# An attention stage with its selections, a mixer split and a variance moved between blocks, and unread products added on TensorE

## The reference, cut to what matters

```
def diff_attention(q, k, v, lam, lam_init, subln_g):        # 4 heads, two maps each
        logits = einsum(qblk, k) * scale + bias              # distance bias, causal by chunks of 64
        p = softmax(where(allowed, logits, -inf))
        attn = p[:, :, 0] - lam * p[:, :, 1]
        return einsum(attn, v)
    o = rms_norm_2(o, subln_g) * (1.0 - lam_init)            # per head of 128

def dsa_attention(q, k, v, qi, ki, wi):                      # 4 heads of 64
        score = einsum(wi * idx_scale, relu(einsum(qi, ki)))
        _, sel = lax.top_k(score, topk)                      # 256 keys of each query
        ...softmax over the selected keys only
```

## Time and profile before

| | us |
|---|---|
| median of three runs | 2201.16 (2199.04 to 2201.55) |
| the profiled execution, its own time | 2189.69 |
| its span | 2187.9 |
| attention stage, first logits to last values | 1118.6 to 1336.5 |

### The profile page before, as it was taken

One profiled execution on the slowest core, in us unless ns is written; L12 is line 12 of the kernel. 1 busy time (PEld: TensorE's weight loads), 2 busy tenths in 40 slices (PEclk: granted clock), 3 DMA queues, 4 the chain that ended last, 5 costly groups with the idle time before them and its releaser, 6 DMA issues.

```text
span 2187.9 us, 25880 instructions
## 1 busy us (share of the span) xinstructions
PE 2108.8 (96%) x9834; PEld 1694.3 (77%) x9834; DVE 1100.7 (50%) x1708; ACT 746.3 (34%) x1189; POOL 178.4 (8%) x159
## 2 busy tenths in 40 slices
PE   5999999999999999999988998999999999999998
PEld 4888888878888887588855667878788888888877
DVE  7743463664234373878888764483412222222146
ACT  3311124432112443655755654242111111111133
POOL 1000002300000231012210000310000000000000
PEclk6999999999999999999978999999999999999999
DMA  8433333222111422101110002221111111111131
GB/s 301 144 118 95 105 105 87 77 68 70 45 48 48 135 81 87 51 21 29 49 39 1 1 1 106 87 77 53 54 49 48 45 56 50 40 48 58 46 127 77
DMA packets 222092, 154.75 MB, mean 71 GB/s; under 512 B 6565, under 2 KB 209462, under 8 KB 221878
## 3 DMA queue, kind: packets, MB, share of 16 engines
q1 hardware_dynamic: 215392, 134.53, 20.1%
q0 software_dynamic: 4608, 16.78, 2.3%
q10 hardware_dynamic: 2006, 2.31, 0.3%
HBM read 145.21 MB, written 8.39 MB: 70 GB/s over the span
## 4 chain that ended last, share of the span: by engine, by line
PE 82%; DVE 9%; ACT 6%; issue 2%; DMA 1%; POOL 0%; ACTq 0%; DVEq 0%; POOLq 0%; SPq 0%
PE pair L2084 36%; PE pair L2101 17%; PE pair L2534 8%; PE pair L2287 4%; PE pair L2142 3%; PE pair L2421 3%; ACT proj L996 2%; PE pair L2389 2%; PE pair L2320 2%; PE pair L2604 1%; PE pair L2403 1%; PE pair L2308 1%; PE pair L2113 1%; DVE act_region L1698 1%; DVE w_lo L1321 1%
## 5 line engine op out<-in xcount | busy, mean ns | idle before, releaser
L1327 DVE TENSOR_TENSOR w_lo<-w_raw,w_hi 128x1024 fp32r<-128x1024 f32 x101 | 123.8, 1225 | 672.0 <-ACT w_hi L780 671.8
L780 ACT ACTIVATE w_hi<-w_raw 128x1024 fp32r<-128x1024 f32 x102 | 108.2, 1061 | 804.1 <-PE pair L2084 623.0
L2084 PE MATMUL pair<-act_hi,w_hi 128*128 128x512 f32 x1168 | 361.3, 390 | 1.8 <-ACT v_all L936 1.8
L2084 PE MATMUL pair<-act_lo,w_hi 128*128 128x512 f32 x1168 | 359.6, 389 | 0.0
L2084 PE MATMUL pair<-act_hi,w_lo 128*128 128x512 f32 x1168 | 359.6, 389 | 0.0
L2084 PEld LDWEIGHTS pair<-act_hi,w_hi 128*128 128x128 f32 x1168 | 218.9, 188 | 48.8 <-ACT v_all L936 2.2
L2084 PEld LDWEIGHTS pair<-act_hi,w_lo 128*128 128x128 f32 x1168 | 219.2, 188 | 45.7
L2084 PEld LDWEIGHTS pair<-act_lo,w_hi 128*128 128x128 f32 x1168 | 219.2, 188 | 45.6
L2101 PE MATMUL pair<-act_hi,w_hi 128*128 128x512 f32 x608 | 243.9, 401 | 4.2 <-DVE act_lo L1340 2.0
L2101 PE MATMUL pair<-act_lo,w_hi 128*128 128x512 f32 x608 | 237.7, 391 | 0.0
L2101 PE MATMUL pair<-act_hi,w_lo 128*128 128x512 f32 x608 | 237.6, 391 | 0.0
(11 more groups left out here) (407 smaller groups left out, 3157.5 us busy)
## 6 DMA issues: line engine op xcount, KB each, us to landing
w_raw<-w_in SPq DMA_DIRECT2D x76, 512.0 KB, 3.7
w_raw<-w_out SPq DMA_DIRECT2D x48, 512.0 KB, 3.8
w_raw<-w_gu SPq DMA_DIRECT2D x48, 512.0 KB, 3.7
w_raw<-w_down SPq DMA_DIRECT2D x24, 384.0 KB, 3.0
act_region<-w_ada SPq DMA_DIRECT2D x16, 512.0 KB, 13.4
sq<-w_ada POOLq DMA_DIRECT2D x16, 512.0 KB, 3.8
sq_sum<-w_ada POOLq DMA_DIRECT2D x16, 512.0 KB, 4.9
yT<-x SPq DMA_DIRECT2D x8, 512.0 KB, 7.4
```

Of the source, the lines that this page charges most:

```text
L780: A(w_hi[s_][:], w_raw[s_][:], ACT.Copy).then_inc(hi_ready, 1)
L1327: v.tensor_tensor(w_lo[s_][:], w_raw[s_][:], f32(w_hi[s_][:]), ALU.subtract)\
L2084: i = mm(bank[pair][:, h * HALF:(h + 1) * HALF], w[slot][:, k, :], a[:, k, h * HALF:(h + 1) * HALF], start=(k == 0 and w is w_hi and a is ...
```

## The change

Four things are done, all around the attention loop.

1. Tiles 4, 5, 6 and 7 are selected in blocks 2, 3, 5 and 6 (`SELECT_IN`) instead of 0, 1, 2 and 3; the scratch is a row of `act_region` that is free then.
2. The mixer's split goes to block 7: ACT makes piece `it` at the end of iteration `it` of that block, behind `turned(k)`, and DVE its piece at the end of its own iteration, behind `combine(k)`, waiting for ACT's. The variance and scale of the first four blocks go from block 4 to block 7, too.
3. POOL makes `w_lo` of units 14 and 15 only after seven blocks' `c_out` (`c_taken`), and ACT makes `w_hi` of unit 15 behind the copy of unit 13. The loads of the next two weight pieces, which wait for POOL's parts, follow.
4. PE runs 14 more products, of 128x128 by 512 columns in FP32 (`keep_busy`), into half a bank pair that nothing reads: two ahead of the loop, and one in each of the twelve iterations of blocks 0 and 1, between `values(k-1)` and `turn(k)`.

```diff
+SELECT_IN = {2: 4, 3: 5, 5: 6, 6: 7}
...
-            for n in range(5, N_UNITS + 2):
+            for n in range(5, N_UNITS):
+                unit_lo(n)
+            pool.wait_ge(c_taken, TT - 1)
+            for n in range(N_UNITS, N_UNITS + 2):
                 unit_lo(n)
...
             for n in range(2, N_UNITS):
-                unit_hi(n + 2)
+                if n < N_UNITS - 1:
+                    unit_hi(n + 2)
+                else:
+                    act.wait_ge(unit_done, 1 + U_PROJ + n + 2)
...
+            unit_hi(N_UNITS + 1)
...
             exps(0)
-            for b in range(2):
-                for a in range(2):
-                    A(act_hi[:, b, a * HALF:(a + 1) * HALF], proj[:, S_AU + b, a * HALF:(a + 1) * HALF], ACT.Copy)\
-                        .then_inc(s_hi, 1)
             for k in range(N_ITEMS):
...
-                if k == 4 * ITEMS + 2:
+                if i == TT - 1 and it < MIX_CHUNKS:
+                    b, a = divmod(it, 2)
+                    act.wait_ge(sel_done, N_TS)
+                    A(act_hi[:, b, a * HALF:(a + 1) * HALF], proj[:, S_AU + b, a * HALF:(a + 1) * HALF], ACT.Copy)\
+                        .then_inc(s_hi, 1)
+                if k == 7 * ITEMS + 2:
                     act.wait_ge(ob_var, 1)
                     A(o_ss[:, tiles(0)], o_ss[:, tiles(0)], ACT.Sqrt).then_inc(ob_rstd, 1)
...
-                same = junk[:, 0:n] if i in EARLY_SEL else proj[:, S_AU, 0:n]
+                same = junk[:, 0:n] if i in EARLY_SEL else act_region[:, 0, 0:n]
...
-                if SEL0 + len(EARLY_SEL) + i < TT:
-                    select(SEL0 + len(EARLY_SEL) + i, it)
-                if k < MIX_CHUNKS:
-                    b, a = divmod(k, 2)
-                    dve.wait_ge(s_hi, SP_MIX + k + 1)
+                if i in SELECT_IN:
+                    select(SELECT_IN[i], it)
+                if i == TT - 1 and it < MIX_CHUNKS:
+                    b, a = divmod(it, 2)
+                    dve.wait_ge(s_hi, SP_MIX + it + 1)
...
-                if k == 4 * ITEMS + 1:
+                if k == 7 * ITEMS + 1:
                     ob_variance(0)
-                if k == 4 * ITEMS + 4:
+                if k == 7 * ITEMS + 4:
                     ob_scale(0)
+            dve.wait_ge(pool_lo, N_UNITS + 2)
+            dve.sem_inc(lo_ready, N_UNITS + 2)
...
+            def keep_busy():
+
+                mm(bank[2][:, half(1)], identity[:], dist_bias[:, half(0)], start=True, stop=True)
+
             logits(0)
             logits(1)
+            pe.wait_ge(dist_ready, 1)
+            keep_busy()
+            keep_busy()
             for k in range(N_ITEMS):
...
                 if k:
                     values(k - 1, groups_of(k - 1) - 1)
+                if i < 2:
+                    keep_busy()
                 if groups_of(k) == 2:
                     turn(k, 0)
```

More of the change, by code:

```diff
@@ L1777, in _ @@
                                     f32(act_hi[:, b, a * HALF:(a + 1) * HALF]), ALU.subtract).then_inc(s_lo, 1)
-                if k == MIX_CHUNKS:
-                    dve.wait_ge(pool_lo, N_UNITS + 2)
-                    dve.sem_inc(lo_ready, N_UNITS + 2)
                 if i and it == 0:
```

## The result

The changed kernel takes 2214.9 us (median of 4 runs, 2214.4 to 2216.2). The kernel before took 2201.0 beside it (2199.0 to 2201.6). The ratio is 1.0072, with a 95% interval from 1.0059 to 1.0085: slower by 0.7%. The profiled execution of the changed kernel took 2215.04 us, with a span of 2213.2.

A forecast was written before the change was run, and what follows sets the result against it. DVE bounds blocks 0 to 3, PE blocks 5 and 6. Terms -13.7 + 2.8 + 17.0 + 1.0 + 6.8 = +13.9 took the profiled 2189.7 to 2203.6; adding 11.5 gave 2215 us, range 2203 to 2226.

The forecast's parts named there:

- part 5: Block 7: PE, ACT and DVE run one after the other; +17.0 us, and +1.0 for POOL holding up DVE.
- part 6: Block 7: PE's clock falls behind each of four idle stretches, 1.7 us lost each; +6.8 us (0 to 10).
- parts 1 and 2: Entry gains 1.9 us, blocks 0 and 1 gain 7.1, with block 0 iterations of 1.9 us; 9.0 together.
- part 3: Blocks 2, 3, 4: smaller tiles gain 1.7 and 1.5 us in full, variance and scale leaving block 4 gain 1.5.
- part 4: Blocks 5 and 6: selection steps that don't fit DVE's free time cost +2.8 us (0 to 4).
- Behind attention: After the attention stage: clock full there, so nothing can move by this change; 0 us.
- The last step of the sum: Whole kernel: 2203.6 us for the profiled execution, plus 11.5 by which the kernel before's median exceeded its profile, gives 2215.
- Two of the prediction's signs: Block 7: DVE waits four times for ACT's split, 3 to 5 us each; the block grows by 18 to 25 us.
- That the waits cost no clock: Block 7: low clock passes while PE is idle; +7 us in sum, 2208 us; chance 0.14.
- Faster, only the first wait is paid: Block 7: PE pays 4.3 us once and the clock stays; -6.5 us, 2195 us; chance 0.13.
- that rival: Blocks 0 and 1: unread products don't hold the clock, some 10 us lost instead of 7 gained; 2232 us; chance 0.06.
- The draw: Attention: gains at upper bound (18) against block 7 at its lower (14); within 4 us of before; chance 0.12.

The follow-up runs named there:

- the attempt to steady that kernel: Kernel before with two unread products added in the last item of block 3: 2195.0 us, ratio 0.9992.
- the unchained kernel: Changed kernel, but DVE makes its four mixer pieces in one go in item 46, behind the last biased and the scale: 2187.6 us, ratio 0.9964.
- The two versions put together from the blocks: Changed kernel with DVE's mixer pieces in item 46, selections in blocks 0, 1, 3, 6, variance and scale in block 5: 2185.7 us with unread products, 2189.5 without.

## Why the prediction was right, and where it only seemed so

**Block 7's chain (part 5): right, with its sizes.** DVE waits four times for ACT's piece, 24.4 us in all, 4.2 to 8.0 each where the prediction had 3 to 5. PE's first `logits` behind the chain is 4.2 us late for 4.3. With the clock held full, the transposes of item 46 are 18.8 us late, where the prediction had 18.0 (17.0 + 1.0) for the copy of that item; the three products ahead of them may have a share in the 18.8. The variance and scale, counted at 1.2 and 0, cost 1.9 to 2.1 in block 7 of the kernels without the chain, at full clock; their share in the chained one no run shows. The 1.0 for POOL's lock was right in kind: the step of 0.22 us took 1.87 between POOL's 1297.20 and 1301.87, 1.65 longer, on an instruction of DVE with SBUF inputs only. The `biased` instructions beside it ran at 0.68 to 0.75 us, as they do without POOL, as the prediction took it. By the rule that it cited (the Trainium skill, SBUF — State Buffer, "Who interferes with whom"), the trace agrees. That the lock was gone from the entry shows too: 0.75 us where the earlier trace rows has 2.82:

```profile
1117.12 0.75 DVE L1688 SCALAR_TENSOR_TENSOR buf_b<-buf_b,cnt,junk 128x512 f32<-128x512 f32 x1
```

**The clock in block 7 (part 6): right in kind, too small, and wrong in form.** I had four falls of 1.7 us each, 6.8. Measured are 13.4 us by the two medians and 11.7 by the spans; by the stretches 11.8 in block 7 and 1.1 behind it. I took each fall to last as long as the one behind attention. By the same comparison (22.6 us late for the last transposes of item 46 with the falls, 18.8 without) the first three cost 3.8 us together. The fourth, behind a stand of 4.17 us, lasted from about 1340 to past 1366 and cost 8.0: the 32 value matmuls of 64 columns took 6.79 and 6.93 us instead of 3.68. The first matmuls behind a wait ran at the lower level (2.08 us instead of 1.13). By the rule on bursts parted by waits (the Trainium skill, TensorE: Matmul & The Clock Gate, "HAM oscillation — how this bites in real kernels"), the trace agrees.

**Blocks 0 and 1 with the entry (parts 1 and 2): the right sum for half a reason.** 9.0 us were predicted and 9.0 measured, between these two traces, and the iteration of block 0 was 1.83 us for 1.9. `c_out` of block 1 stands 34.8 us behind the first `logits`; I had said about 35. But the prediction reads as if the products had a share in the gain. By its own numbers 1.75 us of PE work stood at the low clock and 1.75 at the full one with a product, and the conclusion from that, that they are worth nothing where DVE isn't late, wasn't drawn. The run without them measured it. Part of the 9.0 is also the execution that stood for the kernel before: from the end of the last projection unit to the `c_out` of block 1 the same instructions took 44.9 us in it and 41.1 in the attempt to steady that kernel, where the clock didn't fall a second time. The changed kernel took 35.9, so against that trace the gain is 5.2.

**Blocks 2 to 4 (part 3): 3.7 us instead of 4.7.** Block 4 gave 1.8 for 1.5. Blocks 2 and 3 gave 0.9 and 1.0 for 1.7 and 1.5. "Gained in full" was the wrong step. DVE was nearly gapless there, but what it lost in work didn't all come off the stretch; where the missing 1.3 us went no run shows.

**Blocks 5 and 6 (part 4): 3.2 for 2.8.** Block 5 lost 1.7, block 6, read in the unchained kernel, 1.5 (36.10 against 34.62).

**Behind attention: missed.** The prediction began with a clock that is full everywhere but in attention, so that nothing outside could move, and 2.9 us were lost there. In part that is the low clock of block 7, which reaches 8.8 us past the last `c_out`, where the kernel before has a fall of 3.4 us. The rest goes with a further fall of the clock, some 135 us behind the last `c_out`. The stretch in the changed kernel, then the same place in the kernel before:

```profile
1494.00:1500.00 6.00, 5.67 (x18) 4.61 (x19) 4.90 (x8) 2.17 (x3) 0.00 (x0) 0.72 0.32 90
```

```profile
1471.00:1477.00 6.00, 6.00 (x28) 4.94 (x27) 4.25 (x7) 2.18 (x3) 0.00 (x0) 1.00 0.30 90
```

The change isn't shown to bring it. The two versions put together from the blocks run the same instructions there; the one with unread products has full clock at that place and takes 851.4 us behind attention, the other has 0.72 and takes 854.0 (a part of that is its longer fall right behind the last `c_out`).

**The last step of the sum was wrong.** I added 11.5 us because the runs of the kernel before lay that far above its profiled execution, and said that nothing in the change scales with the difference. But the changed kernel's runs lie within 1.2 us of its profiled one. A second trace of the kernel before shows one fall of the clock inside attention, worth 6.2 us, at a place where the changed kernel has full clock in its profile. How much of the 11.5 that fall makes in the longer runs isn't shown, since they weren't profiled. So the sum for the profile should have been 25.3, not 13.9, and the addition 0. The 11.4 us that the sum lacked are 5.7 in block 7 (30.5 for 24.8, with the first wait counted to it), 2.9 behind attention, 1.4 ahead of it, 1.0 in blocks 2 to 4 and 0.4 in blocks 5 and 6. Both errors were some 11.5 us, with opposite signs, and that is why 2215.0 met 2214.9: luck. The direction and the place stand on the experiments; the last digits don't. Two of the prediction's signs also missed: DVE's waits, and block 7, which grew by 26.3 us where it had 18 to 25.

**The rivals.** That the waits cost no clock is out (12 to 13 us). "Faster, only the first wait is paid" is out: the delay grew by 4.9, 4.6 and 4.1 us an item. The kernel that really has no chain takes 2187.6. The clock was held in blocks 0 and 1, so that rival is out. Its price, products at the low clock, stays untested; without products blocks 0 and 1 took 33.3 us, less than with them, although the clock fell. The draw is out, too: the gains were 12.7 us up to block 4, and block 7 cost 30.5.

## What to carry to other kernels

An in-order engine's free time isn't a place to put work in: 5 us of work that waited in the wrong place cost 27 us more than the same instructions behind everything that others waited for, where they cost 0.5 to 1.8 us of block 7. Before placing a step, write down whom it waits for, what is queued behind it, and whether that queue feeds the engine at the start of the wait; if it does, the three engines go in a circle and the overlap is gone.

Price an idle stretch of TensorE twice, once for itself and once for the clock behind it, and don't take the second from one short example: the first three falls here cost 3.8 us together, the fourth 8.0. Filler products aren't free either. In this kernel they paid in the stands of block 7, and in blocks 0 and 1 only beside selections on DVE; where TensorE itself was next in line they cost a little more than they gave.

When the median of a kernel lies above its profiled execution, find out where before carrying that difference over to another version. It may be a place that the change removes.

## What the hardware showed that I had not expected

The clock stayed at the lower level for some 27 us with TensorE busy in 20.87 of 24 us, while its work was mostly transposes and value products of 64 columns in FP32. It was at the full level again three us after the split products of 512 columns began. That those brought it back is a guess: in the second trace of the kernel before it also rose inside attention, between 1214 and 1220, and attention has no such products. Changed kernel, the first of them and one after the rise:

```profile
1364.86 0.78 PE L2109 MATMUL pair<-act_hi,w_hi 128*128 128x512 f32 x1
...
1369.17 0.39 PE L2109 MATMUL pair<-act_hi,w_hi 128*128 128x512 f32 x1
```

The same was seen in block 0 without unread products: 14 us at 0.50, PE busy in 13.08 of them. And it was seen in the kernel before, 18 us at 0.50 with PE busy 17.95, in one execution and not in another. So once at the lower level this kernel's attention can stay there for long with hardly a stand of PE, and the same code can take one way or the other. With stands of 1.21 us in the last items and a full clock to start from, the clock didn't fall (kernel before and the kernel with fillers in block 7, values at 3.68 us). Why it falls at the head of block 4 only in some executions, behind stands that were equal in both to 0.01 us, no run here settles.
